# Attention's output multiplied by its inverse root ahead of its split, and the MLP norm's sum over partitions as two rounded parts

## What is computed

```
o = chunk_causal_attention(q_nope, q_pe, ..., k_nope, kpe_keys, v, ...)
merged = concatenate([rmsnorm(o.reshape(B, T, ATTN_W), attn_out_g), rmsnorm(y_lru, lru_out_g)])
h = x + merged @ w_out
f = square(relu(rmsnorm(h, norm_mlp_g) @ w_up)) @ w_down
return h + f
```

## Time and profile before

| | us |
|---|---|
| median of 3 runs (2450.86 to 2453.57) | 2450.87 |
| the profiled execution | 2451.89 |
| its span, first to last instruction | 2450.0 |
| TensorE busy | 2436.3 (99%) |
| VectorE busy | 1807.3 (74%) |
| ScalarE busy | 1287.9 (53%) |

### The profile page before, as it was taken

How to read it: one execution, slowest core, us unless ns; L and a number is a source line. 1 busy time by engine, 2 the same in 40 slices (tenths; PEclk the granted TensorE clock), 3 DMA queues, 4 the chain that set the end, 5 groups by cost and what they waited for, 6 DMA issues and landing times.

```text
span 2450.0 us, 44424 instructions
## 1 busy us (share of the span) xinstructions
PE 2436.3 (99%) x17462; PEld 2350.8 (96%) x17462; DVE 1807.3 (74%) x2892; ACT 1287.9 (53%) x2313; POOL 538.8 (22%) x513
## 2 busy tenths in 40 slices
PE   9999999999999999999999999999999999999998
PEld 9999977899999999999999999779999999999998
DVE  8677767778776677677676787677787766776676
ACT  5566355655554455455525763557455544554454
POOL 0024155200112211220201142542002112211222
PEclk9999999999999999999999999999999999999999
DMA  4232100453447634764731222005435456545655
GB/s 163 71 115 73 53 11 20 87 154 107 96 86 137 129 86 95 137 118 89 221 98 52 61 73 53 11 20 113 137 107 115 87 114 132 110 87 119 132 107 181
DMA packets 109741, 242.50 MB, mean 99 GB/s; under 512 B 15536, under 2 KB 18960, under 8 KB 109408
## 3 DMA queue, kind: packets, MB, share of 16 engines
q0 software_dynamic: 48512, 102.26, 23.3%
q1 hardware_dynamic: 60880, 137.37, 17.9%
q10 hardware_dynamic: 144, 0.04, 0.0%
HBM read 147.39 MB, written 94.29 MB: 99 GB/s over the span
## 4 chain that ended last, share of the span: by engine, by line
PE 94%; DVE 3%; DMA 1%; issue 1%; ACT 0%; POOL 0%; SPq 0%; DVEq 0%; POOLq 0%; ACTq 0%
PE ps L1074 24%; PE ps L1500 24%; PE ps L1549 23%; PE ps L1320 5%; PE ps L1335 4%; PE ps L1393 3%; PE ps L1641 3%; PE ps L1434 2%; PE ps L1267 2%; PE ps L1292 1%; PE ps L1612 1%; PE ps L1198 1%; DMA x_scratch<-stage 1%; DMA draw<-in_wst 0%; DVE mxp L2828 0%
## 5 line engine op out<-in xcount | busy, mean ns | idle before, releaser
L3225 DVE TENSOR_TENSOR wlo<-raw_all,whi 128x512 fp32r<-128x512 f32 (+1 forms) x420 | 270.9, 653 | 180.6 <-ACT whi L2267 178.0
L2267 ACT ACTIVATE whi<-raw_all 128x512 fp32r<-128x512 f32 (+1 forms) x420 | 249.1, 601 | 277.6 <-DVE raw_all L3358 88.2
L3747 POOL DMA_DIRECT2D x_scratch<-stage x224 | 200.5, 945 | 838.2 <-DVE stage L3368 693.1
L2320 ACT ACTIVATE stage<-ps 128x536 f32<-128x536 f32 (+1 forms) x224 | 135.6, 613 | 148.8 <-PE ps L1549 143.2
L3368 DVE TENSOR_TENSOR stage<-stage,ps 128x536 f32<-128x536 f32 (+1 forms) x168 | 118.9, 708 | 85.5 <-PE ps L1549 83.9
L2828 DVE TENSOR_REDUCE mxp<-ps 64x1 f32<-64x64 f32 (+11 forms) x384 | 140.4, 372 | 54.8 <-PE ps L1267 48.3
L1074 PE MATMUL ps<-xgh,whi 128*128 128x358 f32 (+1 forms) x720 | 157.2, 326 | 0.0
L1074 PE MATMUL ps<-xgl,whi 128*128 128x358 f32 (+1 forms) x720 | 156.6, 325 | 0.0
L1074 PE MATMUL ps<-xgh,wlo 128*128 128x358 f32 (+1 forms) x720 | 156.5, 325 | 0.0
L1697 ACT ACTIVATE whi<-raw_all 128x1024 fp32r<-128x1024 f32 (+3 forms) x64 | 58.2, 909 | 174.6 <-PE ps L1074 158.0
L1074 PEld LDWEIGHTS ps<-xgl,whi 128*128 128x128 f32 x720 | 124.0, 189 | 0.0
(11 more groups left out here) (949 smaller groups left out, 7792.4 us busy)
## 6 DMA issues: line engine op xcount, KB each, us to landing
raw_all<-in_wst SPq DMA_DIRECT2D x237, 256.0 KB, 3.4
raw_all<-in_wst SPq DMA_DIRECT2D x74, 512.0 KB, 3.6
x_scratch<-stage POOLq DMA_DIRECT2D x120, 268.0 KB, 6.0
x_scratch<-stage POOLq DMA_DIRECT2D x120, 264.0 KB, 6.0
xall<-x_scratch SPq DMA_DIRECT2D x32, 537.0 KB, 8.5
x_scratch<-xall POOLq DMA_DIRECT2D x24, 537.0 KB, 3.3
raw_all<-in_wst POOLq DMA_DIRECT2D x30, 256.0 KB, 4.8
xall<-in_xT SPq DMA_DIRECT2D x8, 537.0 KB, 8.6
```

The costliest lines, as they stand in the source:

```text
L2267: nc.scalar.activation(dst, src, ACT.Copy).then_inc(S["u_hi"], 1)
L2320: nc.scalar.activation(quarters(stage_of(L, g, i, n)[:, 0:N2]), src, ACT.Copy, scale=-1.0 if row else 1.0).then_inc(S["x_copy"], 1)
L3225: V.tensor_tensor(dst, src, hi.bitcast(F32), ALU.subtract).then_inc(S["u_lo"], 1)
L3747: pool.dma_start(x_scr[2 * i + row, :, a:b], stage_of(L, g, i, n)[:, 0:b - a], accum_op=ALU.add).then_inc(S[done], 16)
```

## The change

The inverse root now multiplies `o` itself: `o_normal(j)` on VectorE, ahead of `o_high` and `o_low`. The sum of squares has to be ready before, so its chain moves up: `divide(3)` comes one place after y_block_sum(2, 1), o_add(2) and o_add(3) directly behind one another, and TensorE's sum stands behind P5(2). Its rest goes to bank 5, P2(2) waits for the logarithm, and the logarithm and the exponential are separate steps on ScalarE. The eight multiplies by `rs` behind the attention products are gone: VectorE adds PSUM to x in one operation, and PSUM slots are freed by that add. The MLP norm's sum is split in two rounded parts (`xss_hi` by ScalarE, `xss_lo` by VectorE, in the place of squares no longer needed), and summed by `sum_of_parts`. Per-layer counts of semaphores and the names of the new tiles are left out below.

```diff
@@ -248,7 +248,7 @@
 for _c in range(8):
-    READ[U_OO + _c] = ("oo_ev", _c + 1)
+    READ[U_OO + _c] = ("res_add", _c + 1)
 for _c in range(10):
@@ -675,7 +676,7 @@
             if n in (SUM_O, SUM_MLP):
-                return ps[:, 1 if n == SUM_O else 5, CH:CH + b - a - SUM_END]
+                return ps[:, 5, CH:CH + b - a - SUM_END]
             return ps[:, 3 * slot_of(sum_at(n, layer)) + 2, CH:CH + b - a - SUM_END]
@@ -1045,7 +1046,6 @@
                         w("y_copy", y_copied(u - U_OO + 2, "P4"))
                         w("y_add", y_added(3, "P3"))
-                        w("root", SUM_O)
                         return
                     if u in U_XR[2:4] and L == 0:
@@ -1364,6 +1364,8 @@
                     elif name == "P2":
                         dst = pair_slot(3, L)
+                        if p == 2:
+                            w("root", SUM_O)
                         if p:
                             w("y_add", y_added(p - 1, "P2"))
@@ -1397,10 +1399,10 @@
                     for name in Y_ORDER:
                         y_product(p, name)
-                        if (p, name) == (NYP - 1, "P7"):
+                        if (p, name) == (2, "P5"):
                             w("sum_lo", SUM_O)
-                            w("y_add", y_added(p, "P2"))
-                            w("y_copy", y_copied(p - 1, "P4"))
+                            w("y_add", y_added(1, "P2"))
+                            w("y_copy", y_copied(1, "P4"))
                             sum_of_parts(SUM_O, osqt_r, osq_r)
                 for m in range(8):
@@ -1437,14 +1439,14 @@
                 pe.wait_ge(S["u_lo"], L * PER["u_lo"] + 2)
-                pe.wait_ge(S["oo_ev"], L * PER["oo_ev"] + 7)
+                pe.wait_ge(S["res_add"], L * PER["res_add"] + 7)
                 first_up(0, range(6), False)
-                pe.wait_ge(S["oo_ev"], L * PER["oo_ev"] + 8)
+                pe.wait_ge(S["res_add"], L * PER["res_add"] + 8)
                 first_up(1, range(6), False)
...
                 first_up(1, (6, 7), True)
-                pe.wait_ge(S["xm_sum"], L * PER["xm_sum"] + 7)
-                sum_of_squares(SUM_MLP, xss)
+                w("sum_lo", SUM_MLP)
+                sum_of_parts(SUM_MLP, xss_hi, xss_lo)
                 pe.wait_ge(S["u_lo"], L * PER["u_lo"] + 4)
@@ -1761,14 +1763,23 @@
-                def log_rstd(n, dst, dim):
+                def log_sum(n, dst, dim):
...
                     nc.scalar.activation(dst[:, a + SUM_END:b], sum_rest(n, L), ACT.Ln, scale=1.0 / dim, bias=eps[:, 0:1]).then_inc(S["root"], 1)
+
+                def exp_root(n, dst):
+
                     w("root", n)
+                    a, b = sum_cols(n, L)
                     nc.scalar.activation(dst[:, a:b], dst[:, a:b], ACT.Exp, scale=-0.5).then_inc(S["rstd"], 1)
+
+                def log_rstd(n, dst, dim):
+
+                    log_sum(n, dst, dim)
+                    exp_root(n, dst)
@@ -2038,55 +2049,57 @@
                 def o_high(j):
+                    w("o_n", j + 1)
+                    nc.scalar.activation(live(oh[j]), live(o[j]), ACT.Copy, scale=col(V_AG + j)).then_inc(S["o_hi"], 1)
+
+                def o_square(j):
+
                     w("o", j + 1)
-                    nc.scalar.activation(live(oh[j]), live(o[j]), ACT.Copy, scale=col(V_AG + j)).then_inc(S["o_hi"], 1)
-
-                def o_square(j):
-
                     if j >= 2:
                         w("o_sum", j - 1)
...
                 w("pv", NH * NP)
                 y_copy(0, "P1")
-                o_high(0)
+                o_square(0)
                 y_copy(0, "P5")
                 y_fill_hi(1, 0)
                 y_copy(0, "P6")
-                o_square(0)
+                o_square(1)
                 y_fill_hi(1, 1)
-                o_high(1)
-                o_square(1)
                 y_copy(0, "P4")
                 y_fill_hi(1, 2)
                 y_copy(1, "P1")
                 y_fill_hi(1, 3)
+                o_square(2)
                 y_copy(1, "P5")
                 y_fill_hi(2, 0)
                 y_copy(1, "P6")
-                o_high(2)
                 y_fill_hi(2, 1)
-                o_square(2)
+                o_square(3)
                 y_fill_hi(2, 2)
+                w("o_sum", 3)
+                nc.scalar.activation(live(osqt_r), live(osq), ACT.Copy).then_inc(S["sum_hi"], 1)
                 y_copy(1, "P4")
                 y_fill_hi(2, 3)
                 y_copy(2, "P1")
-                o_high(3)
                 y_copy(2, "P5")
                 y_fill_hi(3, 0)
+                log_sum(SUM_O, rs, ATT)
                 y_copy(2, "P6")
-                o_square(3)
+                exp_root(SUM_O, rs)
                 y_fill_hi(3, 1)
                 y_fill_hi(3, 2)
                 y_copy(2, "P4")
                 y_fill_hi(3, 3)
+                o_high(0)
                 y_copy(3, "P1")
-                w("o_sum", 3)
-                nc.scalar.activation(live(osqt_r), live(osq), ACT.Copy).then_inc(S["sum_hi"], 1)
+                o_high(1)
                 y_copy(3, "P5")
                 split(B_OO)
                 y_copy(3, "P6")
-                log_rstd(SUM_O, rs, ATT)
+                o_high(2)
+                o_high(3)
                 split(B_OO + 1)
                 y_copy(3, "P4")
@@ -2201,6 +2214,8 @@
                     w("res_add", 8)
+                    w("xm_sum", 7)
+                    nc.scalar.activation(xss_hi[:, A0:TOK], xss[:, A0:TOK], ACT.Copy).then_inc(S["sum_hi"], 1)
                     copy_out(at, 0, True)
@@ -2996,7 +3011,6 @@
                     w("o_hi", j + 1)
-                    w("o_sq", j + 1)
                     lo(live(ol[j]), live(o[j]), live(oh[j]), "o_lo", col(V_AG + j))
@@ -3009,52 +3023,62 @@
                     V.tensor_tensor(live(osq), live(osq), live(osqt), ALU.add).then_inc(S["o_sum"], 1)
+                def o_normal(j):
+
+                    w("rstd", SUM_O)
+                    w("o_sq", j + 1)
+                    V.tensor_tensor(live(o[j]), live(o[j]), live(rs), ALU.mult).then_inc(S["o_n"], 1)
+
+                invert(3)
                 y_fill_lo(1, 0)
                 y_block_sum(1, 1)
-                invert(3)
                 y_add(0, "P2")
                 y_add(0, "P7")
...
                 y_block_sum(1, 3)
                 y_add(0, "P3")
-                o_low(0)
+                o_add(1)
                 y_fill_lo(1, 2)
                 y_block_sum(2, 0)
-                o_add(1)
                 y_fill_lo(1, 3)
                 y_fill_lo(2, 0)
                 y_block_sum(2, 1)
-                o_low(1)
+                divide(3)
                 y_add(1, "P2")
                 y_add(1, "P7")
...
                 y_block_sum(2, 2)
                 y_block_sum(2, 3)
+                o_add(2)
+                o_add(3)
                 y_add(1, "P3")
-                divide(3)
                 y_fill_lo(2, 2)
+                sum_lo(osq_r, osq, osqt_r, SUM_O)
                 y_block_sum(3, 0)
-                o_add(2)
                 y_fill_lo(2, 3)
                 y_fill_lo(3, 0)
                 y_block_sum(3, 1)
-                o_low(2)
                 y_add(2, "P2")
                 y_add(2, "P7")
...
                 y_block_sum(3, 2)
                 y_block_sum(3, 3)
-                o_add(3)
                 y_add(2, "P3")
+                o_normal(0)
                 y_fill_lo(3, 2)
+                o_normal(1)
                 y_fill_lo(3, 3)
-                o_low(3)
-                sum_lo(osq_r, osq, osqt_r, SUM_O)
+                o_low(0)
+                o_normal(2)
                 split(B_OO)
+                o_normal(3)
                 y_add(3, "P2")
                 y_add(3, "P7")
+                o_low(1)
                 y_add(3, "P3")
+                o_low(2)
+                o_low(3)
                 split(B_OO + 1)
@@ -3090,8 +3114,6 @@
                         if (name, kk) == ("t3n", 2):
-                            dve.wait_ge(S["xm_sum"], L * PER["xm_sum"] + 7)
-                        if (name, kk) == ("t3n", 3):
                             w("sum", SUM_MLP)
@@ -3121,15 +3143,12 @@
                 for i, m in enumerate(OO_ORDER):
-                    if i == 0:
-                        w("rstd", SUM_O)
                     if i == 6:
...
                         up_lo(0, 1)
-                    scaled(U_OO + i, osqt, rs, "oo_ev", LIVE)
-                    w("oo_ev", i + 1)
                     w(f"x_in{m}", 32)
-                    V.tensor_tensor(live(x[m]), live(x[m]), live(osqt), ALU.add).then_inc(S["res_add"], 1)
+                    w("mm", U_OO + i + 1)
+                    V.tensor_tensor(chunks(x[m], LIVE), chunks(x[m], LIVE), slot(U_OO + i, LIVE), ALU.add).then_inc(S["res_add"], 1)
                     w("res_add", i + 1)
@@ -3147,7 +3166,11 @@
                 in_sum(7)
-                for name, kk in F_ORDER[2:]:
+                for name, kk in F_ORDER[2:4]:
```

(4 more changed lines are left out.)

9 lines of the change are left out of this document (5 added, 4 removed).

## The result

The changed kernel takes **2461.05 us** (median of 6 runs, 2459.84 to 2462.53) where the kernel before, run beside it, takes 2450.86 (6 runs, 2449.92 to 2453.57): ratio **1.0042**, 95% interval 1.0032 to 1.0052. It is slower, by 10.2 us; forecast was 2460.7, with slower at 91%. The profiled execution took 2460.59 us with a span of 2458.8, so 8.7 us above the profiled one of before.

The account below looks back on a forecast made before the run. TensorE, almost without waits, was taken as the bound, so late inputs add in full. 5.0 us (layer 1) + 5.4 (layer 2) - 0.6 (MLP) = +9.8 us, giving a median of 2460.7 us; 80% range 2457.3 to 2464.7.

Parts of the forecast that it names:

- Wait 2.65: y products, per layer: P5(2) waits for VectorE's y add queued behind the sum-of-squares chain, starting at 484.5 instead of 481.9.
- Wait 0.65: y products: P4(1) waits for VectorE's add for P7(1), behind the division and its broadcast, starting at 478.85 instead of 478.2.
- Wait 0.3: y products: attention's sum waits 0.3 us for its low part, ready at 486.25 while P5(2) ends at 486.05.
- Wait 1.15: y products: P2(2) waits 1.15 us for ScalarE's logarithm, because it writes the banks of attention's sum.
- Wait 0.2: End of the y stage: y_add(3, "P3"), behind multiplies and low parts on VectorE, ends late; a wait of 0.2 us.
- The clock rival: TensorE's 2.65 us wait drops its clock to 1.2 GHz, for one product a layer 2 x 1.5 us: 2463.7 us; chance 4%.
- The table load: ScalarE, ahead of the logarithm: the load takes 1.30 us, now on the path, where before it ran ahead and cost nothing.
- The second look's drain: By the skill page, some 1.38 us more per table load: 2.8 us over both layers, 2463.5 us in all.
- The MLP's -0.6: MLP norm's sum in rounded parts: 0.81 us less TensorE work per layer, 0.3 kept, -0.6 us in all.
- The multiplies behind the attention products worth nothing there: Attention products: taking eight full-width multiplies per layer off VectorE gains nothing, since TensorE waits for none of them.

Follow-up runs that it names:

- the filled version: The changed kernel with 24 dummy matmuls put ahead of P5(2) in TensorE's queue, inside its wait: 2460.48 us, ratio to before 1.0037.

## Why the prediction was right

- **The sum against the result.** Forecast 2461.7 us for the profiled execution and 2460.7 for the median; measured 2460.59 and 2461.05. The y stage came 11.0 us longer over both layers, where the forecast had 10.4. Part of the match is luck: in layer 1 the waits of 0.65 and 1.15 did not come, and slower matmuls (1.4 us), which the sum did not have, came in their place; in layer 2 the slower matmuls came on top.
- **"Wait 2.65" at P5(2)**, the largest term: 2.53 and 2.51 us, on the add, the cause as named. Taking the square's wait away took it down to 1.3, and moving the add only moved it to the sum.
- **"Wait 0.65" at P4(1)**: not in layer 1, and 0.1 us in layer 2. The broadcast took 6.9 us, not the 7.4 I took from the earlier trace rows, and the division started at 475.43 instead of 476.2. The term depends on that landing; with later landings in layer 2 it is there, with 0.68 in the filled version and 0.80 with the MLP's part undone.
- **"Wait 0.3" at the sum**: there in layer 1 with some 0.2 us, too short for the list of waits. The low part of the sum of squares ends at 485.54 and the sum starts at 485.59; in the filled version it starts 0.05 us behind that end in both layers. In layer 2 P5(2), at half clock, took 2.71 us and covered it.
- **"Wait 1.15" for the logarithm**: absent in layer 1, 0.93 in layer 2. In layer 1 the sum took 1.1 us and P6(2) some 0.55 longer than at the full clock before (of which 0.2 is there in the filled version as well), and P2(2) came 0.3 us after the logarithm's end. The filled version has this wait in both layers, with 0.96 and 0.97, so the term was about right in size and was covered in layer 1 by something dearer.
- **"Wait 0.2" at the end**: the first attention product starts some 0.25 us behind TensorE's pace, 0.26 after y_add(3, "P3") ended. In all seven versions with the sum moved, and in both layers, it starts 0.25 to 0.27 us behind that add, so the add is what it waits for.
- **The clock rival** got 4%, and its mechanism came about in both layers. I was wrong to leave its chance that low on the ground that no row had a wait so long. Its price was of the right order: I put it at 3 us in all, for one product per layer; the matmuls were 1.4 and 1.3 us slower, and 1.5 us in all reached the end. So the rival is part of the result, beside the forecast's terms and not instead of them. The Trainium skill ("TensorE: Matmul & The Clock Gate", section "HAM oscillation — how this bites in real kernels") warns of waits in mid-kernel; the trace agrees, with 1.00 falling to 0.50 behind a wait of 2.5 us.
- **The table load.** The exponential started 1.29 us after its load did, and the logarithm 1.29 us after its own, although that one stands directly behind a fill. The second look's drain, which would have made 2463.5 us, is not there in the new place either. The Trainium skill ("ScalarE: Activation LUTs", section "What ACT_TABLE_LOAD costs") has 1.38 us more; here the measurement decides.
- **The MLP's -0.6**: -0.62, and its split was right too. I had VectorE get 1.2 and shed 1.3 + 0.2 per layer. The low part alone costs 1.2, and taking the multiplies out beside it brings 1.5 (26.96 to 25.44 us), which makes the -0.3. Without the rounded sum the same multiplies bring only 0.1 to 0.2: no wait for VectorE is left there then, and TensorE's own work ends last.
- **The multiplies behind the attention products worth nothing there**: shown, ratio 1.0 without them on the kernel before.
- **Still open**: the 0.3 to 0.5 us per layer lost between P2(2) and the first attention product. Some 0.25 to 0.3 of it is the wait for y_add(3, "P3") above, behind low parts and multiplies on VectorE; the rest, some 0.1 to 0.2, has no cause in the rows, and no version took the multiplies off that queue.

## What to carry to other kernels

Before an operation is moved forward in the busiest engine's queue, write down when its inputs are ready and what stands behind the waits that this adds in the other queues: here 0.8 us less matmul work per layer was sought, and a y stage longer by 4.9 and 6.2 us came with it. A part that is worth nothing or costs time alone can pay in company, so measure parts in both ways, taken out of the change and put alone on the old kernel. And a wait costs more than its length when the clock falls behind it; here dummy matmuls in the wait kept the clock full, and the stage lengths put the gain at 1.5 us, though the median's 0.6 can't be told from none.

## What was not expected of the hardware

- The half clock followed on a single wait of TensorE, in a stretch that is otherwise busy throughout, in five cases: 2.53 and 2.51 us in the changed kernel, 2.51 in layer 2 with the MLP's part undone, 3.10 and 3.35 with y's add first, where it lasted over 6 us. One wait of 2.35 us, and several of 1.3 to 1.6, left it full. In the changed kernel the clock fell when TensorE was already at work again, with y's add first in the last part of the wait.
- The broadcasts of rc and the weight blocks land at times that differ from execution to execution of nearly the same program, 6.6 to 7.7 us for the slower of the first and 9.0 to 10.6 for the third weight block, and each was on or near TensorE's path: this moved a layer by up to about 1 us.
- What lies outside the three stages of the table, summed over the execution, differed by up to 3 us between profiles (2215.2 to 2218.2), so a single pair of spans would not have shown the terms of this size; stage lengths did.
